# Five further products behind each norm's statistics, in a three-block transformer on one Trainium2 core

## The reference

```python
def layer_norm(x, g, b):
    xf = x.astype(jnp.float32)
    mu = jnp.mean(xf, axis=-1, keepdims=True)
    var = jnp.mean(jnp.square(xf - mu), axis=-1, keepdims=True)
    y = (xf - mu) * lax.rsqrt(var + LN_EPS)
    return (y * g.astype(jnp.float32) + b.astype(jnp.float32)).astype(x.dtype)
...
        x = layer_norm(DN_ALPHA * x + 0.5 * swiglu_ffn(x, ffn1_wg[i], ffn1_wu[i], ffn1_wd[i]),
...
        x = layer_norm(DN_ALPHA * x + y, ln2_g[i], ln2_b[i])
```

## Time and profile before

| | us |
|---|---|
| median of 3 runs | 3102.16 (3097.86 to 3105.52) |
| the profiled execution | 3101.18 |
| its span | 3099.4 |
| TensorE busy (matmul records) | 2867.2, 93% |
| GpSimd busy | 1180.8, 38% |
| VectorE busy | 1079.5, 35% |
| ScalarE busy | 1020.5, 33% |

### The profile page before, as it was taken

One profiled execution on the slowest core, in us unless ns is written; L12 is line 12 of the kernel. 1 busy time (PEld: TensorE's weight loads), 2 busy tenths in 40 slices (PEclk: granted clock), 3 DMA queues, 4 the chain that ended last, 5 costly groups with the idle time before them and its releaser, 6 DMA issues. The chain is left out here.

```text
span 3099.4 us, 35532 instructions
## 1 busy us (share of the span) xinstructions
PE 2867.2 (93%) x14186; PEld 2254.8 (73%) x14186; DVE 1079.5 (35%) x1761; ACT 1020.5 (33%) x1493; POOL 1180.8 (38%) x396
## 2 busy tenths in 40 slices
PE   8999999999889998889999799778899989999998
PEld 6887788887689677668878587255687736778876
DVE  2110215997434542241110401556503335621103
ACT  3331232233544424342221321244323435332212
POOL 4444453444363256254444441111242211554443
PEclk9999999999999999989999899888899989999999
DMA  4222232233200323122222223200222110222221
GB/s 156 97 101 88 82 121 81 95 137 127 89 1 2 143 88 123 41 82 95 95 95 95 82 95 151 77 28 14 102 95 96 55 51 31 79 95 95 96 94 68
DMA packets 41574, 266.50 MB, mean 86 GB/s; under 512 B 4208, under 2 KB 5616, under 8 KB 13168
## 3 DMA queue, kind: packets, MB, share of 16 engines
q1 hardware_dynamic: 37856, 256.47, 22.6%
q10 hardware_dynamic: 3600, 8.39, 0.7%
HBM read 248.07 MB, written 16.78 MB: 85 GB/s over the span
## 5 line engine op out<-in xcount | busy, mean ns | idle before, releaser
L210 POOL TENSOR_TENSOR weights_lo<-weights_raw,weights_hi 128x2048 fp32r<-128x2048 f32 x196 | 918.4, 4686 | 1561.8 <-ACT weights_hi L199 1561.8
L240 PE MATMUL psum<-x_hi,weights_hi 128*128 128x512 f32 (+1 forms) x2368 | 938.7, 396 | 80.9 <-DVE x_lo L360 35.4
L241 PE MATMUL psum<-x_lo,weights_hi 128*128 128x512 f32 (+1 forms) x2368 | 927.2, 392 | 0.0
L242 PE MATMUL psum<-x_hi,weights_lo 128*128 128x512 f32 (+1 forms) x2368 | 927.0, 391 | 0.0
L199 ACT ACTIVATE weights_hi<-weights_raw 128x2048 fp32r<-128x2048 f32 x202 | 386.6, 1914 | 784.3 <-PE psum L242 703.8
L240 PEld LDWEIGHTS psum<-x_hi,weights_hi 128*128 128x128 f32 x2368 | 453.6, 192 | 199.1 <-issue 84.6
L242 PEld LDWEIGHTS psum<-x_hi,weights_lo 128*128 128x128 f32 x2368 | 452.8, 191 | 94.3
L241 PEld LDWEIGHTS psum<-x_lo,weights_hi 128*128 128x128 f32 x2368 | 454.2, 192 | 90.0 <-issue 0.2
L416 DVE SCALAR_TENSOR_TENSOR arena<-arena,psum 128x512 f32<-128x512 f32 x66 | 45.4, 687 | 567.3 <-PE psum L242 567.3
L240 PE MATMUL psum<-h_hi,weights_hi 128*128 (+1 forms) x528 | 207.7, 393 | 7.3 <-PEq L381 7.3
L241 PE MATMUL psum<-h_lo,weights_hi 128*128 (+1 forms) x528 | 206.0, 390 | 0.0
(11 more groups left out here) (324 smaller groups left out, 3395.6 us busy)
## 6 DMA issues: line engine op xcount, KB each, us to landing
weights_raw<-in_stream SPq DMA_DIRECT2D x202, 1024.0 KB, 4.8
keep_gates<-arena ACTq DMA_DIRECT2D x24, 256.0 KB, 2.0
arena<-keep_gates SPq DMA_DIRECT2D x3, 2048.0 KB, 9.6
arena<-keep_x SPq DMA_DIRECT2D x3, 2048.0 KB, 8.4
keep_x<-arena SPq DMA_DIRECT2D x2, 2048.0 KB, 9.8
arena<-in_w_k SPq DMA_DIRECT2D x2, 2048.0 KB, 8.4
arena<-in_na_bias SPq DMA_DIRECT2D x1, 3584.0 KB, 12.4
arena<-in_x_t SPq DMA_DIRECT2D x2, 1024.0 KB, 8.0
```

What stands on the lines that cost most here:

```text
L210: K.nc.gpsimd.tensor_tensor(K.wlo[:, 1 - slot, :, :], K.raw[:, 1 - slot, :, :], K.whi[:, 1 - slot, :, :].bitcast(F32), ALU.subtract).then_ ...
L240: K.nc.tensor.matmul(out, whi, xhi, start=start, stop=False)
L241: K.nc.tensor.matmul(out, whi, xlo, start=False, stop=False)
L242: return K.nc.tensor.matmul(out, wlo, xhi, start=False, stop=stop)
```

## The change

Behind the four statistics products of `pe_last`, TensorE does five more of the same kind, with the squares of chunks 0 to 4 as moving operand, each one starting bank 6 anew. They update no semaphore, and nothing reads what they write.

```diff
@@ -566,6 +566,8 @@
         mm(mean, K.mat("mean"), self.chunk(7), start=False, stop=True).then_inc(s("mean_ready").sem, s("mean_ready").n())
         pe.wait_ge(s("squared").sem, s("squared").at(8))
         mm(var, K.mat("mean"), self.squares[:, 7, :], start=False, stop=True).then_inc(s("var_ready").sem, s("var_ready").n())
+        for c in range(5):
+            mm(K.ps[:, 6, :], K.mat("mean"), self.squares[:, c, :], start=True, stop=True)
 
     def square(self, act, chunks):
         s = self.K.s
```

## The result

The changed kernel takes 3113.05 us (median of 5, 3112.69 to 3117.31) against 3102.16 before; the ratio is 1.0042, with a 95% interval from 1.0030 to 1.0054. In a second comparison it came out at 3117.32 against 3102.73, ratio 1.0046 (1.0033 to 1.0059). It is slower, by 13 to 14 us in the mean of the executions. The forecast was 3110, within 0.3%. The profiled execution took 3113.05 us, its span is 3111.3.

What follows compares the result with a forecast made beforehand. TensorE, busy for 93% of the span, was taken to bound the kernel. Barriers add 8.9 us and the clock returns 1.0, so +7.9 us on 3102.16, predicted median 3110, range 3103 to 3115.

Steps and rivals of the forecast that it cites:

- What is added: Behind the `var` product at six places: five products of 0.86 us, 4.30 us in all, ending before TensorE reaches the barrier.
- The sum at the barrier: At six norm stage ends: 1.44 us exposed at each of five, 1.72 at the last, together 8.9 us.
- The crossing: From the last engine's end, over the stage's closing barrier, to the next stage's first step: 0.34 us.
- The spare time of 2.86 us: End of `ffn1_out`, standing for five places: TensorE's last statistics product ends 2.86 us before GpSimd's half tile.
- Nothing later takes this up … so the whole rest of the program moves: Behind each late barrier: every engine and SyncE's next load start later, so the 8.9 us stay in full.
- the four restarts: TensorE's first products after `ffn1_out`, `mix_out`, `xo`, `out_3`; 18.0 us at half clock before, 16 forecast.
- What the clock may give back: After four norm ends: shorter TensorE idle time cuts half clock from 18.0 to 16 us, returning 1.0 us.
- two mean clocks below 0.75: Ten microseconds behind each restart: mean clock 0.77 to 0.83 expected; 1.0 or below 0.75 would show the prediction wrong.
- TensorE is busy throughout these stretches, so it pays: Ten microseconds behind four restarts: half of the 18.0 us at half clock, 9.0 us, counted as lost time.
- the clock gives nothing or takes: Rival at four restarts: 5.6 us at half clock each, 2.2 us lost, 11.1 us slower, 3113.3; chance 0.12.
- The full clock: Rival at four restarts: the shorter gap keeps the clock full, 9.0 us come back, 3102.1; chance 0.10.
- The products ran at full clock: Against the rival that added products run at half clock, 4.3 us more per place, 3137; chance 0.03.

Runs made afterwards that it cites:

- the kernels with three or five products and the fill: Kernel before plus three or five products at six places, and four (three in `xk`) heading TensorE's list in four following stages; 3103.79 and 3106.32 us.
- the kernel with the fill alone: Kernel before plus only products heading TensorE's list in `glu`, `ffn2_in`, `ffn3_in` (four each) and `xk` (three); 3100.34 us, ratio 0.9994.

## Why the prediction was wrong

- **What is added**: right. Ten records, 4.30 us, full clock, behind the last statistics product, and in front of the barrier.
- **The sum at the barrier**: right. 8.9 us forecast, 8.6 measured; 1.38 and 1.71 us per place for 1.44 and 1.72. The crossing is 0.29 us with TensorE last in place of 0.34. The spare time of 2.86 us is shown from both sides, by three products (nothing) and four (0.5).
- **"Nothing later takes this up … so the whole rest of the program moves"**: this is the step that failed. The rest moved, but it did not stay as long as it was. 4 to 5 us of the 13 to 14 come from stages in which the change has no instruction, or from the norm's stages beside the barrier, where more of the half clock fell under work (198.1 us in place of 190.9 in the mean of the profiles). The forecast had put the clock's answer at the four restarts alone, and at nothing elsewhere. Why the sum elsewhere is a loss stays open.
- **What the clock may give back**: forecast 1.0 us, and the four stages were 0.84 us shorter in the mean of the profiles, but that it is so near is luck. The idle times were as said, 4.1 and 3.5 us, and the clock fell. But half clock lasted 18.2 us in place of the 16 forecast, with two mean clocks below 0.75, so that by the prediction's own price nothing would have come back. And it was priced at half its length, which is too much: GpSimd's low parts bound the first tile, so that full clock at all four restarts was worth 4.4 us and not 9.0. Nor does the idle time fix the answer: after the same 4.1 us the kernels with six and ten products had 14 to 15 us at half clock. "TensorE is busy throughout these stretches, so it pays" drew a bound from a busy share; the wait comes behind the stretch.
- **The rivals**: "the clock gives nothing or takes" was nearest in time, 3113.3 against 3113.05, but not by its mechanism: two of the four restarts had its 5.6 us at half clock, and yet the four stages together lost nothing. The full clock did not come about, and was not worth its price. The products ran at full clock.
- **The numbers**: 3113.05 lies within 3103 to 3115, the second comparison's 3117.32 does not. The range had no room for a cost outside the change's own stages, and "within 0.3%" had 0.64 for that reason.

The advice of the Trainium skill, page "TensorE: Matmul & The Clock Gate", section "Why this matters for your kernels", to leave no idle gap between bursts holds for the clock itself in the kernels with three or five products and the fill, where it stayed at 1.00 behind the four restarts. The gain was decided here by who bounds the work behind the gap, GpSimd.

## What to carry to other kernels

Work that nobody waits for is free only up to the moment at which its engine becomes the last at the next barrier; read the spare time of that engine there before adding any, and put the filler behind the barrier, where its engine waits anyway; it must end there in time at half clock too, for in three places of the kernel with the fill alone it did not and held the restart back by 1 us. Before booking a gain from a faster clock, look who feeds the engine behind the gap: at full clock it may just wait. And a shift of a few microseconds can change where the clock falls in stages that no edit touches, by as much as the effect that one wants to measure, so compare stage by stage over several profiles.

## What was not expected of the hardware

The clock can fall under full work: in `in_2` it was full at the restart after 3.92 us of idle time and fell 1.3 us later, and in the changed kernel's restart in `ffn2_in`, after 4.11 us, it fell within a microsecond of it. After 3.20 us of idle time it fell too, in three of four places, about 1 us behind the first product. The same idle time of 4.1 us was followed by 0.71 in one kernel and by 0.84 in another. The same stage with the same records takes one of two times, 199.0 or 202.2 us, and an execution of the same program 3097 to 3109.
